# Two of the 24 weight halves of each pair of expert blocks multiplied unsplit, as f32, from one 8 KB buffer

## The reference

```python
for each block of rows xe of one expert e:
    gu = xe @ w_gate_up[e] + b_gate_up[e]        # 1024 x 2048 weights
    gate = minimum(gu[..., 0::2], 7);  up = clip(gu[..., 1::2], -7, 7)
    act = (up + 1) * (gate * sigmoid(1.702 * gate))
    y = act @ w_down[e] + b_down[e]              # 1024 x 1024 weights
out[row_tok] += y * row_gate
```

## Time and profile before

| | |
|---|---|
| median of 3 runs | 1439.85 us (1437.68 to 1439.9) |
| the profiled execution's own time | 1438.17 us |
| its span (first to last instruction) | 1436.5 us |
| busy share of the span: PE, DVE, ACT, POOL | 93%, 89%, 72%, 30% |
| splits of weights on DVE (L991) | 411, 2284 ns each |
| splits of weights on ACT (L639) | 411, 1919 ns each |
| weights fetched | 396 halves of experts, 1 MB each |

### The profile page before, as it was taken

How to read it: one execution, slowest core, us unless ns; L and a number is a source line. 1 busy time by engine, 2 the same in 40 slices (tenths; PEclk the granted TensorE clock), 3 DMA queues, 4 the chain that set the end, 5 groups by cost and what they waited for, 6 DMA issues and landing times.

```text
span 1436.5 us, 20084 instructions
## 1 busy us (share of the span) xinstructions
PE 1333.8 (93%) x6418; PEld 1058.0 (74%) x6418; DVE 1282.2 (89%) x1252; ACT 1029.2 (72%) x941; POOL 426.8 (30%) x282
## 2 busy tenths in 40 slices
PE   6999989889999999999999899999999999999996
PEld 5876866776777777777877777777777777788883
DVE  7348565789999999999999999999999999999998
ACT  5344444537788888878787888888887878877772
POOL 0000000024343536243443335343535434311100
PEclk9999999899999999999999999999999999999998
DMA  9411130279999999999999999999999999999994
GB/s 353 159 60 59 34 147 16 77 262 385 398 399 401 400 390 398 406 392 403 400 406 394 397 394 398 394 391 405 399 400 397 404 394 395 391 378 377 368 371 178
DMA packets 102341, 472.82 MB, mean 329 GB/s; under 512 B 16499, under 2 KB 16539, under 8 KB 68000
## 3 DMA queue, kind: packets, MB, share of 16 engines
q1 hardware_dynamic: 87632, 451.79, 79.6%
q0 software_dynamic: 14672, 20.53, 4.1%
HBM read 467.78 MB, written 22.02 MB: 341 GB/s over the span
## 4 chain that ended last, share of the span: by engine, by line
PE 44%; DVE 24%; issue 14%; DMA 9%; ACT 8%; DVEq 0%; SPq 0%; ACTq 0%
DVE w_lo L991 13%; PE gu_bank L1529 9%; PE gu_bank L1531 9%; PE gu_bank L1530 9%; DMA raw<-in_w_down_dram 8%; ACT w_hi L639 6%; DVE arena L1373 2%; PE turn_bank L1529 2%; PE turn_bank L1531 2%; PE turn_bank L1530 2%; PE bank L1529 2%; DVE arena L1383 1%; ACT turned L815 1%; PE bank L1531 1%; PE bank L1530 1%
## 5 line engine op out<-in xcount | busy, mean ns | idle before, releaser
L991 DVE TENSOR_TENSOR w_lo<-raw,w_hi 128x2048 fp32r<-128x2048 f32 x411 | 921.5, 2284 | 69.6 <-ACT w_hi L639 68.6
L639 ACT ACTIVATE w_hi<-raw 128x2048 fp32r<-128x2048 f32 x411 | 776.4, 1919 | 131.7 <-PE gu_bank L1531 98.9
L601 POOL DMA_INDIRECT expert_rows<-arena x32 | 222.4, 6949 | 331.4 <-ACT arena L840 172.3
L1529 PE MATMUL gu_bank<-w_hi,turned 128*128 128x512 f32 x632 | 251.9, 399 | 12.3 <-DVE w_lo L991 8.3
L1531 PE MATMUL gu_bank<-w_hi,turned 128*128 128x512 f32 x632 | 247.0, 391 | 0.0
L1530 PE MATMUL gu_bank<-w_lo,turned 128*128 128x512 f32 x632 | 247.0, 391 | 0.0
L1535 PE MATMUL gu_bank<-w_hi,turned 128*128 128x512 f32 x448 | 179.9, 402 | 29.6 <-DVE w_lo L991 28.2
L1536 PE MATMUL gu_bank<-w_lo,turned 128*128 128x512 f32 x448 | 175.1, 391 | 0.0
L1529 PEld LDWEIGHTS gu_bank<-w_hi,turned 128*128 128x128 f32 x632 | 119.0, 188 | 47.6 <-DVE w_lo L991 16.9
L1531 PEld LDWEIGHTS gu_bank<-w_hi,turned 128*128 128x128 f32 x632 | 119.0, 188 | 25.4
L1530 PEld LDWEIGHTS gu_bank<-w_lo,turned 128*128 128x128 f32 x632 | 119.1, 188 | 23.2
(11 more groups left out here) (339 smaller groups left out, 1766.6 us busy)
## 6 DMA issues: line engine op xcount, KB each, us to landing
raw<-in_w_gate_up_dram SPq DMA_DIRECT2D x264, 1024.0 KB, 11.2
raw<-in_w_down_dram SPq DMA_DIRECT2D x132, 1024.0 KB, 9.1
raw<-in_w_in_dram SPq DMA_DIRECT2D x10, 1024.0 KB, 8.3
raw<-in_w_out_dram SPq DMA_DIRECT2D x4, 1024.0 KB, 6.1
raw<-expert_rows SPq DMA_DIRECT2D x4, 1024.0 KB, 6.6
raw<-in_w_mem_kv_dram SPq DMA_DIRECT2D x2, 1024.0 KB, 12.3
arena<-in_x_dram SPq DMA_DIRECT2D x1, 2048.0 KB, 13.8
arena<-in_position_tables_dram SPq DMA_DIRECT2D x1, 2048.0 KB, 17.5
```

The source lines that it names most:

```text
L601: pool.indirect_dma_start(y_dram, bass.IndirectOffsetOnAxis(idx_scatter, 0), y_row, None, bounds_check=TOPK * S - 1, oob_is_err=False).the ...
L639: a.activation(home, raw_ap, ACT.Copy).then_inc(hi_ready, 1)
L991: v.tensor_tensor(home[1], raw_ap, home[0].bitcast(F32), ALU.subtract).then_inc(lo_ready, 1)
L1529: pe.matmul(bank, a[0], b[0], start=first, stop=False)
```

## The change

In each pair two halves are no longer split. They are the gate/up slice k = 5 of the wide block (WHOLE_GU) and down half j = 0 of the wide block (WHOLE_DN), which PE uses in the body of the next narrow block. Each is fetched into `spare`, one buffer of 8 KB a partition in the arena, and PE multiplies it as plain f32: four matmuls of 512 columns instead of twelve. ACT keeps an f32 copy of the turned rows or activations these matmuls need (`keep_x`, 128x128, and `keep_act`, 128x256). ACT and DVE skip the two halves, and the counters are advanced by two at the half before. SP's loop becomes a loop over pairs; the slice k = 5 is issued after k = 7, the down half after k = 5, each behind a wait for the spare's last reader; the skipped raw slot stays empty for a turn. The last-needed gains and biases, whose home the spare takes, are loaded by POOL after block 29's step, behind a wait for the last f32 gate/up slice.

```diff
+WHOLE_GU, WHOLE_DN = 5, 0
+        spare = F[:, 11264:13312]
+        x_whole, act_whole = F[:, 13568:13568 + P], F[:, 13696:13696 + 2 * P]
 # SP
+            def skip_slot(i, free):
+                sp.wait_ge(lo_ready, free)
+                sp.sem_inc(raw_in[i % 6], 16)
+            def narrow_after_wide(b):
+                before, e = experts_of(b)
+                for k in range(GU):
+                    gate_up(e, k, GU + k, b * 12 + (7 + k))
+                    if k == 5:
+                        sp.wait_ge(half_used, b * 12 + 6)
+                        sp.dma_start(spare.rearrange("p (k n) -> p k n", k=2),
+                                     dn_dram[bass.ds(before, 1), :, 2 * WHOLE_DN:2 * WHOLE_DN + 2, :]
+                                     .rearrange("e p k n -> p (e k) n")).then_inc(whole_dn_in, 16)
+                for j in range(DN):
+                    if j == WHOLE_DN:
+                        skip_slot(2 * GU + j, b * 12 + (7 + GU + j))
+                    else:
+                        down(before, j, 2 * GU + j, b * 12 + (7 + GU + j))
+            def wide_after_narrow(b):
+                before, e = experts_of(b)
+                for k in range(GU):
+                    if k == WHOLE_GU:
+                        skip_slot(GU + k, b * 12 + (7 + k))
+                    else:
+                        gate_up(e, k, GU + k, b * 12 + (7 + k))
+                sp.wait_ge(half_used, b * 12 + (1 + GU + WHOLE_DN))
+                sp.dma_start(spare.rearrange("p (e n) -> p e n", e=1),
+                             gu_dram[bass.ds(e, 1), :, WHOLE_GU, :].rearrange("e p n -> p e n")).then_inc(whole_gu_in, 16)
+                for j in range(DN):
+                    down(before, j, 2 * GU + j, b * 12 + (7 + GU + j))
 # POOL: the five gf_in transfers go from here ...
-            pool.dma_start(g_final, ...).then_inc(gf_in, 16)
 # ... to between two loops of its steps
+            steps(2, LOOP_FROM)
+            pool.wait_ge(half_used, (LOOP_FROM - 2) * 12 + (13 + WHOLE_GU))
+            pool.dma_start(g_final, ...).then_inc(gf_in, 16)
 # ACT (DVE alike with lo_m)
+                hi_m(GU + 4, b, 2)         # wide block: k = 5 is skipped
+                hi_m(GU + 6, b)
...
+                keep_act(b)                # narrow block's body
                 turn_act(0, b)
...
+                hi_m(GU + 7, b, 2)         # down 0 is skipped
...
+                keep_x(b + 2)
                 turn_x(0, b + 2)
 # PE
+            def gate_up_whole(n):
+                pe.wait_ge(whole_gu_in, n * 16)
+                for c in range(4):
+                    ins = pe.matmul(psum[c], x_whole, spare[:, c * 512:(c + 1) * 512], start=False, stop=False)
+                ins.then_inc(half_used, 1)
+            def down_whole(n):
+                pe.wait_ge(whole_dn_in, n * 16)
+                for kk in range(2):
+                    for c in range(2):
+                        at0 = kk * D + c * 512
+                        ins = pe.matmul(psum[4 + c], act_whole[:, kk * P:(kk + 1) * P], spare[:, at0:at0 + 512],
+                                        start=kk == 0, stop=False)
+                ins.then_inc(half_used, 1)
```

## The result

The changed kernel takes 1455.19 us (median of four runs, 1452.06 to 1456.87) against 1438.87 us for the kernel before in the runs beside it: ratio 1.011, 95% interval 1.0097 to 1.0123. That is 16.3 us more. The prediction said 1450 and slower, so the sign and one of its two mechanisms hold: PE's extra cost was there. But the part that it priced came out smaller than it said, and the larger part of the loss comes from a step that it priced at nothing.

The account below looks back on a forecast made before the run. DVE's list was taken to bound wide-to-narrow stretches, PE narrow-to-wide ones; PE's 1.44 us on 36.26 made 37.70, +11.0 us over the marks, 1449.2 or 1450.9, said as 1450; range 1439 to 1464.

Parts of the forecast that it names:

- The f32 halves on PE: Narrow-to-wide stretch: each unsplit half costs PE 0.72 us more, 1.44 us a pair.
- the sum: Narrow-to-wide stretch without a wait, 36.26 + 1.44 = 37.70 us; wide-to-narrow stays 28.93; +11.0 us over the marks.
- The order of the transfers: SP's queue: k5 late, down half two places early; k6 and k7 land some 2.7 us later, 0 to 1 us once.
- Where the waits before k0 and k1 come from: Narrow-to-wide stretch: PE waits there for DVE's splits after the clamp, 0.65 us on average, all of it let go.
- DVE relieved: Rival: DVE is the bound, a dropped split shortens the wide-to-narrow stretch; -20 us, 1420 us; chance 0.12.
- The transfers as the bound: Rival: transfers set the 65.9 us pair and PE's extra 1.44 us fits into idle time; 1438 to 1442; chance 0.16.
- The late k5: Rival, wide block: PE waits 1.5 us a pair for slice k5, 21 us on top, 1471 us; chance 0.10.
- keep_act, keep_x: ACT's f32 copies: keep_act some 0.35 us, keep_x less; both covered, so nothing; without cover keep_act 5 us.
- the moved transfers: Five transfers of 1 MB in all leave the start and return hidden: nothing, -2 us as a bound.
- The signs: Profile after: stretches 28.9 and 37.7 us, DVE about 59.5 of 66.6 us, about 394 GB/s, no wait for spare.
- The first sign: Profile after: the distance from wide mark to narrow mark is still 28.9 us.

Follow-up runs that it names:

- e_cost: Kernel before, with PE repeating one group of three fp32r products in each of the two halves that the change unsplits: 1443.60 us, ratio 1.0033.
- e_order: Changed kernel with both unsplit halves fetched in the places they had before the change: 1443.67 us, ratio 1.0029.

## Why the prediction came out as it did

*The f32 halves on PE: right.* They show as two groups, 112 records each, eight for each of 14 halves:

```profile
L1886 PE MATMUL turn_bank<-arena 128*128 128x512 f32 x112 | 50.4, 592 | 0.0
L1877 PE MATMUL gu_bank<-arena 128*128 128x512 f32 x112 | 50.3, 592 | 0.0
```

The narrow-to-wide stretch went to 37.37 us, 0.33 less than the 37.70 of the sum. The price was right (37.37 - 35.95 is 1.42, the sum had 1.44); the base was too high: I took the shortest stretch seen, 36.26, for a stretch without waiting, and PE alone needs 35.93. The waiting in the average stretch was 0.98 us, not 0.65. So these stretches give 6.6 us where I had 11.

*The order of the transfers: the step that failed.* It said that k6 and k7 land one place, some 2.7 us, later, and that "with pairs of 66.6 us, longer than the 65.9 that the transfers were running at, they gain that within a few pairs: 0 to 1 us once." They land a place later indeed, and never regain it. It cost 11.4 us by the trace, 0.9 us in each wide-to-narrow stretch, and 11.5 us by the run with the old order. Two things were missing. One is the distance from these landings to the mark, which I never took: k7's is 8.0 to 8.8 us ahead in the kernel before, k6's 2.5 us more, and 7.35 and 9.84 are needed. That leaves 0.7 to 1.4 us, and a place of 2.5 us is more. The other is the assumption that longer pairs let the queue catch up. By the kernel's own waits a late slice is split late, its slot comes free late, and SP issues the next half late: the transfers wait for the same loop that waits for them. (The steady 7.35 us are measured; that this loop is why it isn't made good is read from the code.) In the changed kernel they fall to a share of 0.94 while PE does its 37.36 us, and miss that time later. That k5 and the early half act together (28.93 us for six pairs with only one of them, 29.6 from the first with both) is measured, and so are the 1.3 us of lead that a late k5 takes by itself; that it takes it because SP issues nothing for 9.3 us there is argued, not shown.

*Where the waits before k0 and k1 come from: wrong, and without effect on the sum.* I put them down to DVE's splits after the clamp, because DVE w_lo stands in the bracket. The brackets go one step back. Followed further, DVE waited for ACT and ACT 1.10 us for a down half. The run with fewer bytes shows that all but 0.1 us of this was the transfers'. Since PE's 1.44 us are more than the 0.98 that the transfers held it for, the waits went all the same: in `e_cost` they are gone although no split is dropped. The sum let them go because DVE was relieved, which is the wrong reason.

*DVE relieved: the rival that fell.* The mechanism said 1420 us. The Trainium skill's rule (Perfetto Trace Analysis, section Identifying the Most-Contended Engine) names the engine with the highest occupancy as the one to optimize; for DMA it goes by HBM utilization in place of occupancy, and for TensorE it doesn't trust matmul busy time, which the prediction left out. The dropped splits alone gave 1442.70 us, slower than before. The run went against the half of the rule that the prediction used: occupancy, 64 of 65.9 us, pointed to an engine whose dropped splits are worth 0.06 us a pair once the transfers are out of the way. In the other stretch its list does set the time, 28.9 to 29.1 us in every profile in which the down half isn't fetched early, but none of the dropped splits is in that list, as the prediction said. (That the list sets it is read from the trace, where DVE has no gap; no run shortened the list.)

*The transfers as the bound: nearer than I priced it.* The rival had a share of 1.00 for it, and against it a pair at 415 us with little idle time. It was true of the kernel before, where 13.4 us hang on 1.75 MB a pair. As a forecast it still fails, since with PE's extra 1.44 us a pair in the old order is 66.31 us, just above the 66.17 that the transfers gave without it.

*The late k5: no wait.* PE never waits for the whole half. It is fetched at 837.15 and PE starts on it, without idle time, at 848.72:

```profile
837.15 0.33 SPq L558 DMA_DIRECT2D arena<-in_w_gate_up_dram  x1
```
```profile
848.72 3.59 PE L1877 MATMUL gu_bank<-arena 128*128 128x512 f32 x8
```

The place that I compared it with was the right one, but the queue is so short there that it lands in 6.8 us in the middle (the page's row of these issues), not 8.9.

*keep_act, keep_x, the moved transfers, the tail: nothing each*, as predicted: 28.93 us with the old order of transfers, keep_act's 0.36 us included; 1438.91 us with the move alone; the end after the last mark 193.9 us in both profiles.

*The signs.* DVE's busy time in a pair (59.85 of 66.91 us), the 392 GB/s, the f32 records 0.43 us apart and no wait of PE for the spare all came out as written down. None of them can tell the two causes apart. The first sign, a wide-to-narrow stretch of 28.9 us, failed, and it was said to be wrong only if that stretch shrank; it grew.

In all: +6.6 us where 11 were expected, +11.4 where 0 to 1 were. The errors cancel in part, 4 us down and 11 up, which is why the total looks better than its parts. That 1455 lies near 1450 is luck: with the transfers in their old order the same f32 halves cost 4.6 us by the measured times and 6.4 by the stretches of the profile (`e_order`), where the sum had 11.

## What to carry to other kernels

A wait that the trace puts down to an engine is only its last link: go back link by link, over each bracket, until an engine is found that waits for nothing or for a transfer, before the wait is called that engine's. When DMA reports a share of 1.00, a direct way to see whether it sets the time is to fetch less in the same order and look at the stretches; here it separated three engines that all looked full. And an order of transfers is part of the price of a change: for each transfer that is pushed back, take the distance from its landing to the moment its result is needed, and don't count on a queue to catch up when its buffers are freed by the very work that waits for it.

## What the runs showed of the hardware

A half of 1 MB can land in 4.7 us from its issue when few others are in flight (one slice issued between 836 and 842 us in the changed kernel), so the 11.2 us of the earlier trace rows are mostly queueing behind other halves:

```profile
raw<-in_w_gate_up_dram SPq DMA_DIRECT2D x1, 1024.0 KB, 4.7
```

In the profiles of these kernels halves that are in flight together mostly land 2.46 to 2.56 us apart, and often 3.1 to 3.8 us apart where a gather or scatter of POOL runs between them. By this estimate the 24 halves of a pair are 59 to 61 us at the former rate, and most of the rest of the 65.8 us would be POOL's transfers: the pair stood at the transfers' limit, at a share of 1.00, although its weights alone would have allowed a shorter one. Whether more raw slots, with more halves in flight, would move that limit was not tried; a run with POOL's transfers left out wasn't either.
